# Last output projection in token rows: a per-token norm without a column sum and a spread

## What is computed

```python
def rmsnorm(x, gain):
    y = xf * lax.rsqrt(jnp.mean(xf * xf, axis=-1, keepdims=True) + RMS_EPS)
    return (y * gain.astype(jnp.float32)).astype(x.dtype)

def odd_mixer(h, w_in, pool_w, pool_scale, w_out):
    u, gate = jnp.split(h @ w_in, [POOL_WIDTH], axis=-1)          # 2048 each
    y = multiscale_pool(u, pool_w, pool_scale)
    return (y * jax.nn.silu(gate)) @ w_out                         # 256x2048 @ 2048x1024
...
        x = x + rmsnorm(y, post_norm[layer])                       # the result, 256x1024
```

## Time and profile before

| | us |
|---|---|
| median of 3 runs | 2239.26 (2237.56 to 2242.36) |
| the profiled execution, its own time | 2245.09 |
| its span | 2243.3 |
| PE busy | 2089.1 (93%) |
| PE weight loads busy | 1126.8 (50%) |
| DVE busy | 716.1 (32%) |
| ACT busy | 397.6 (18%) |
| POOL busy | 51.3 (2%) |
| DMA | 572.84 MB, mean 255 GB/s |

### The profile page before, as it was taken

How to read it: one execution, slowest core, us unless ns; L and a number is a source line. 1 busy time by engine, 2 the same in 40 slices (tenths; PEclk the granted TensorE clock), 3 DMA queues, 4 the chain that set the end, 5 groups by cost and what they waited for, 6 DMA issues and landing times.

```text
span 2243.3 us, 26279 instructions
## 1 busy us (share of the span) xinstructions
PE 2089.1 (93%) x10404; PEld 1126.8 (50%) x10404; DVE 716.1 (32%) x1732; ACT 397.6 (18%) x853; POOL 51.3 (2%) x70
## 2 busy tenths in 40 slices
PE   5999999996999999999799899999998999889997
PEld 2345447753334334334466533333333767578886
DVE  3035218625110110112447211111112697710411
ACT  2014210012110110111226211111111232411101
POOL 0000000001000000001000000000000000000000
PEclk9999999997999999999899899999999999798998
DMA  9661219212999999998630399999999633242230
GB/s 361 249 225 38 76 50 368 124 38 91 373 427 414 409 429 411 418 428 362 262 113 17 141 416 428 428 429 427 428 429 414 217 121 96 76 160 94 88 119 19
DMA packets 114475, 572.84 MB, mean 255 GB/s; under 512 B 6112, under 2 KB 20704, under 8 KB 89680
## 3 DMA queue, kind: packets, MB, share of 16 engines
q1 hardware_dynamic: 105280, 541.38, 60.1%
q0 software_dynamic: 6512, 24.67, 3.0%
q10 hardware_dynamic: 2592, 5.51, 0.6%
HBM read 562.88 MB, written 8.65 MB: 255 GB/s over the span
## 4 chain that ended last, share of the span: by engine, by line
PE 77%; DMA 11%; DVE 7%; ACT 2%; issue 2%; SPq 1%; POOL 0%; ACTq 0%; DVEq 0%; POOLq 0%; PEldq 0%
PE banks L516 26%; PE banks L982 7%; PE banks L920 4%; PE banks L960 4%; PE banks L1092 4%; DMA weight_ring<-in_moe_w_up 3%; DMA weight_ring<-in_moe_w_down 3%; PE banks L530 3%; PE banks L728 3%; DMA pages<-h_rows,pages 3%; DVE pages L1902 2%; PE banks L1046 2%; PE banks L937 2%; PE banks L1010 2%; PE banks L1078 2%; PE banks L708 2%
## 5 line engine op out<-in xcount | busy, mean ns | idle before, releaser
L516 PE MATMUL banks<-pages,weight_ring 128*128 128x256 f32 (+1 forms) x2240 | 579.6, 420 | 8.4 <-ACT pages L1601 3.2
L516 PEld LDWEIGHTS banks<-pages,weight_ring 128*128 128x128 f32 x2240 | 429.8, 193 | 157.1 <-issue 103.2
L982 PE MATMUL banks<-weight_ring,pages 128*64 128x512 f32 x992 | 224.0, 597 | 9.7 <-DMA weight_ring<-in_moe_w_gate 5.0
L1686 ACT ACTIVATE pages<-banks 128x512 f32<-128x512 f32 (+1 forms) x150 | 84.3, 572 | 688.6 <-PE banks L862 117.2
L1902 DVE TENSOR_TENSOR pages<-banks,pages 128x512 f32<-128x512 f32 (+3 forms) x165 | 95.4, 619 | 324.0 <-PE banks L890 182.4
L1576 ACT ACTIVATE pages<-banks 128x256 f32<-128x256 f32 (+2 forms) x216 | 91.9, 453 | 597.8 <-PE banks L516 421.7
L920 PE MATMUL banks<-weight_ring,pages 128*64 128x512 f32 x832 | 184.1, 598 | 3.2 <-issue 3.2
L1902 DVE TENSOR_TENSOR pages<-pages 128x512 f32<-128x512 f32 (+9 forms) x306 | 176.2, 598 | 9.2 <-issue 1.1
L1902 DVE TENSOR_TENSOR pages<-pages,banks 128x512 f32<-128x512 f32 (+1 forms) x41 | 28.2, 688 | 410.6 <-PE banks L982 178.0
L982 PEld LDWEIGHTS banks<-weight_ring,pages 128*64 128x64 f32 x992 | 69.0, 137 | 158.1 <-issue 132.5
L1092 PE MATMUL banks<-weight_ring,pages 128*64 128x512 f32 x512 | 114.9, 597 | 6.4 <-DVE pages L2359 5.4
(11 more groups left out here) (297 smaller groups left out, 1828.3 us busy)
## 6 DMA issues: line engine op xcount, KB each, us to landing
weight_ring<-in_moe_w_up SPq DMA_DIRECT2D x64, 2048.0 KB, 19.2
weight_ring<-in_moe_w_down SPq DMA_DIRECT2D x64, 2048.0 KB, 18.6
weight_ring<-in_moe_w_gate SPq DMA_DIRECT2D x62, 2048.0 KB, 17.6
weight_ring<-in_ada_w SPq DMA_DIRECT2D x24, 2048.0 KB, 15.9
weight_ring<-in_even_w_in SPq DMA_DIRECT2D x18, 2048.0 KB, 20.2
weight_ring<-in_odd_w_in SPq DMA_DIRECT2D x8, 2048.0 KB, 8.3
weight_ring<-in_odd_w_out SPq DMA_DIRECT2D x6, 2048.0 KB, 8.9
weight_ring<-in_odd_w_qkv SPq DMA_DIRECT2D x3, 2048.0 KB, 12.7
```

The source lines that it names most:

```text
L516: last = pe.matmul(b[:, 0:w], s[:, k, m * P:(m + 1) * P], src(k)[:, t0:t0 + w], start=(k == 0), stop=(k == nk - 1))
L982: last = pe.matmul(to, xg[:, par, k, 64 * half:64 * half + 64], rows, start=(half == 0 and k == 0), stop=(half == 1 and k == 3))
L1686: act.activation(dst, banks_mem[:, use(l, job)[0], 0:n], func).then_inc(moe_taken(l, job, 0)[0], 1)
```

## The change

- The residual `X` is turned into token rows (`x_tok`, page 2) by 16 PE transposes in four jobs between the pool projection and `out3`; ACT copies the four banks out.
- `out3` takes the activations as the stationary operand (128 tokens) and 256 columns of the weights as the moving one. Chunk c gives two jobs, tokens t = 0 and t = 1, of 128 tokens by 256 features.
- ACT squares each job's bank with a running sum per token into one column of `square_sums`; the squares themselves are not used. DVE multiplies the bank by the gain, which now lies along the row and is a new 128x1024 table (`post_row`), loaded by POOL behind the reciprocals; `recip_loaded` is waited for at 32 in the place of 16.
- In the last chunk, for each t: DVE adds the four sums and scales, ACT takes the root of a 128x1 column, DVE the reciprocal, and then y * r + x in two pieces of 128x512.
- SP stores each piece with a DMA of its own, 256 KB, as soon as it is counted in `x_final`.
- The ones-matmuls, the spread, the eight scalings, the eight adds and the transposes at the end go.

```diff
@@ PE
-        wait_taken(pe, ("pool", ("pool", 0, 3), 3))
-            project("b3o", ("out3", 0, c), lambda k: yp[:, k], 16, 2, NX, n=256)
-        columns_sum("norm_q1", pages(4, 4096).rearrange("p (k t) -> p k t", k=KT), KT, NX)
-        for half in range(2):
-            pe.wait_ge(sem("x_final"), 4 * (half + 1))
-            for s in range(2):
-                job = ("x_out", s, half)
+        for s in range(2):
+            for half in range(2):
+                job = ("x_tok", s, half)
                 b = open_job(job)
                 for k in range(4):
                     last = pe.transpose(b[:, k * P:(k + 1) * P], X[:, 4 * half + k, s * P:(s + 1) * P], ident)
                 close_job(job, last)
+        wait_taken(pe, ("pool", ("pool", 0, 3), 3))
+        for c in range(4):
+            name = ("out3", 0, c)
+            wait_weights(pe, name)
+            w_ = slot(name, 16, 256)
+            for t in range(2):
+                b = open_job(("b3o", name, t))
+                for k in range(16):
+                    last = pe.matmul(b[:, 0:256], yp[:, k, t * P:(t + 1) * P], w_[:, k], start=(k == 0), stop=(k == 15))
+                close_job(("b3o", name, t), last)
+            last_job[name] = ("b3o", name, 1)
@@ SP
-                wait_taken(sp, ("x_out", s, half))
-        sp.dma_start(out[0].rearrange("(s p) n -> p s n", p=P),
-                     pages(2).rearrange("p (s n) -> p s n", s=2)).then_inc(sem("stored"), 16)
-        sp.wait_ge(sem("stored"), 16)
+                sp.wait_ge(sem("x_final"), 2 * s + half + 1)
+                sp.dma_start(out[0, s * P:(s + 1) * P, 512 * half:512 * half + 512],
+                             x_tok[:, s, 512 * half:512 * half + 512]).then_inc(sem("stored"), 16)
+        sp.wait_ge(sem("stored"), 64)
@@ POOL
         put(pages(12, 1024, 1024), tab("recip"), "recip_loaded")
+        put(post_row, tab("post_row"), "recip_loaded")
@@ ACT
+        for s in range(2):
+            for half in range(2):
+                evac(("x_tok", s, half), x_tok[:, s, 512 * half:512 * half + 512])
         for c in range(4):
-            for m in range(2):
-                evac(("b3o", ("out3", 0, c), m), y_raw[:, 2 * c + m], NX)
-        squares("norm_q1", y_raw, 4, NX)
-        root("norm_q1", NX)
+            for t in range(2):
+                b = result(act, ("b3o", ("out3", 0, c), t))
+                act.activation(square_out[:, 2 * c + t], b[:, 0:256], ACT.Square, accum_out=square_sums[:, 4 * t + c:4 * t + c + 1])\
+                    .then_inc(sem("norm_squared"), 1)
+                if c == 3:
+                    act.wait_ge(sem("norm_root"), 2 * NORMS.index("norm_q1") + 2 * t + 1)
+                    act.activation(tok_root[:, t:t + 1], tok_root[:, t:t + 1], ACT.Sqrt).then_inc(sem("norm_root"), 1)
@@ DVE
-        dve.wait_ge(sem("recip_loaded"), 16)
+        dve.wait_ge(sem("recip_loaded"), 32)
...
-        add_normed("norm_q1", vec("post", 8, 8), "x_final")
-        o = pages(2).rearrange("p (s n) -> p s n", s=2)
-        for half in range(2):
-            for s in range(2):
-                evac(("x_out", s, half), o[:, s, 512 * half:512 * half + 512])
+        for c in range(4):
+            for t in range(2):
+                job = ("b3o", ("out3", 0, c), t)
+                cols = slice(256 * c, 256 * c + 256)
+                b = result(dve, job)
+                dve.wait_ge(sem("norm_squared"), KT * NORMS.index("norm_q1") + 2 * c + t + 1)
+                if c == 3:
+                    r = tok_root[:, t:t + 1]
+                    link(dve.reduce_sum(r, square_sums[:, 4 * t:4 * t + 4], AX.X))
+                    dve.tensor_scalar(r, r, 1.0 / D, EPS, ALU.mult, ALU.add).then_inc(sem("norm_root"), 1)
+                y_known = tt(y_tok[:, t, cols], b[:, 0:256], post_row[:, cols], ALU.mult)
+                y_known.then_inc(taken_sem(job), 1)
+                if c == 3:
+                    dve.wait_ge(sem("norm_root"), 2 * NORMS.index("norm_q1") + 2 * t + 2)
+                    link(dve.reciprocal(r, r))
+                    wait_taken(dve, job)
+                    for half in range(2):
+                        wait_taken(dve, ("x_tok", t, half))
+                        cols = slice(512 * half, 512 * half + 512)
+                        dve.scalar_tensor_tensor(x_tok[:, t, cols], y_tok[:, t, cols], r, x_tok[:, t, cols],
+                                                 ALU.mult, ALU.add).then_inc(sem("x_final"), 1)
```

More of the change, by code:

```diff
@@ L76 @@
     ("cos2", 256), ("sin2", 256), ("rot2", 128), ("dilated", 512),
-    ("iota", 256), ("rows", 2), ("recip", 1024),
+    ("iota", 256), ("rows", 2), ("recip", 1024), ("post_row", 1024),
     ("before", 128), ("slots", 512), ("turn", 80)])
@@ L432, in program @@
     y_raw = pages(11).rearrange("p (k t) -> p k t", k=KT)
+    y_tok = pages(11).rearrange("p (s n) -> p s n", s=2)
+    x_tok = pages(2).rearrange("p (s n) -> p s n", s=2)
+    post_row = pages(12, 1024)
+    square_out = pages(10).rearrange("p (i n) -> p i n", i=8)
+    square_sums = S("tiny", 8, 8)
+    tok_root = S("tiny", 0, 2)
     RS = pages(13, 128)
@@ L1359, in _ @@
             project("pool", ("pool", 0, g), lambda k: mixed[:, 4 * g + k], 4, 4, NX)
-        wait_taken(pe, ("pool", ("pool", 0, 3), 3))
-        yp = pages(4, 4096).rearrange("p (j t) -> p j t", j=16)
-        for c in range(4):
-            project("b3o", ("out3", 0, c), lambda k: yp[:, k], 16, 2, NX, n=256)
-        columns_sum("norm_q1", pages(4, 4096).rearrange("p (k t) -> p k t", k=KT), KT, NX)
-        for half in range(2):
-            pe.wait_ge(sem("x_final"), 4 * (half + 1))
-            for s in range(2):
-                job = ("x_out", s, half)
+        for s in range(2):
+            for half in range(2):
+                job = ("x_tok", s, half)
                 b = open_job(job)
@@ L1373, in _ @@
                 close_job(job, last)
+        wait_taken(pe, ("pool", ("pool", 0, 3), 3))
+        yp = pages(4, 4096).rearrange("p (j t) -> p j t", j=16)
+        for c in range(4):
[8 more added lines that the diff above has]
+            last_job[name] = ("b3o", name, 1)
     @block_.sync
@@ L2735, in _ssm, with _tabs @@
     return np.ascontiguousarray(np.concatenate([parts[n] for n in SSM], axis=1))
-def _tabs():
+def _tabs(a):
     t = {}
@@ L2798, in _tabs @@
     t["rows"] = (f[:, None] // 16 % 2 == np.arange(2)[None, :])
+    t["post_row"] = np.broadcast_to(a["post_norm_2"][1], (P, D))
     t["recip"] = np.concatenate(
@@ L2815 @@
     given = {name: np.ascontiguousarray(a[name]) for name in _INS}
-    given["vecs"], given["ssm"], given["tabs"] = _vecs(a), _ssm(a), _tabs()
+    given["vecs"], given["ssm"], given["tabs"] = _vecs(a), _ssm(a), _tabs(a)
     arrays, dram = {}, {}
```

## The result

The changed kernel takes 2225.94 us (median of 5 runs, 2222.52 to 2229.05), the kernel before 2239.26 (5 runs, 2237.56 to 2242.36): a ratio of 0.9939, 95% interval 0.9924 to 0.9954. That is 13.3 us faster by the medians, with an interval of about 10 to 17 us.

A forecast was written before the change was run, and what follows sets the result against it. PE holds 77% of the chain, but nothing remains to overlap in the last 20.85 us. Tail 20.85 - 6.1 = 14.75 saved, less 1.31 for a later projection, gives 13.4 off 2239.26: 2225.9 us, range 2222.4 to 2231.7.

The forecast's parts named there:

- PE ahead of the projection: Before the last projection: sixteen moved transposes take 1.89 us, cover a 0.58 wait for DVE, so it starts 1.31 later.
- The projection: Last projection on PE: 128 matmuls with only the stationary side changed, same time as before, 0 us.
- the rival of an exposed stationary side: Last projection: 256 activation loads of 0.19 us stop hiding beside matmuls, 48.6 us added, 2274.5; chance 2%.
- The new load: 512 KB gain table loaded on POOL, which DVE awaits before pooling: 0 us, with 59 us of cover.
- the four copies: ACT copies of turned residual during the last projection: 2.8 us inside 55.5, nothing on the path.
- the first half's norm: Norm of tokens 0 to 127: 4.3 us beside PE's last job of 6.9 us, costing nothing.
- The tail: From the last matmul's end to the end of the span: 6.1 us in place of 20.85.
- The landing of the last store: Last 256 KB store on SP lands in 2.5 us, bounds 2.2 and 4.0.
- the gain product: After the last matmul's end E, DVE multiplies the bank by the gain in 0.42 us, ending at E + 1.37.
- the dear store: Rival at the end: a 256 KB piece lands only after 4.0 us, gain 11.9, 2227.4; chance 10%.
- the table load: Rival: ACT reloads its table between last square and root, 1.28 us, costing 0.8, gain 12.6, 2226.7; chance 4%.
- The level case: Whole kernel comes out level: the untouched 2166 us before the tail shift by some 9 us; chance 3%.

The follow-up runs named there:

- together run: Changed kernel with the norm of both halves made together after the last matmul: stage (DVE's last pool instruction to span end) 64.50 us, +2.23.

## Why the prediction was right

Forecast 2225.9, measured 2225.94; the faster side, and the mechanism, were as forecast. That the medians meet to a tenth is luck: the stage gained 14.64, not 13.4, and runs differ by several us. From one profiled execution to the other the prediction said 2231.7, and it was 2224.52: 1.2 of the 7.2 us lie in the stage, 6.0 ahead of it, where nothing had been forecast. Step by step:

- *PE ahead of the projection*, 1.31 later: measured 1.01 (1.55 less 0.54), in the changed kernel and alone in the kernel before. The sixteen transposes took 1.75 from the first to the projection's start (2161.98 - 2160.23), 0.109 each at the full clock, in the place of 1.89: the 0.118 of the earlier trace rows counts the last one to its end, as the 1.92 here does. And they begin 0.20 before DVE's instruction (2160.43 - 2160.23), not the 0.04 of the prediction (2166.39 - 2166.35).
- *The projection*, 0: measured 55.42 against 55.52. The rival of an exposed stationary side found nothing: 256 weight loads were hidden beside the matmuls as before.
- *The new load, the four copies, the first half's norm*, 0 each: right, with the covers named; the first half's norm took 3.6 us (2210.53 to 2214.16), not 4.3. The together run shows what the last is worth when its cover is gone: 2.23.
- *The tail*, 6.1: measured 5.30 (2222.7 - 2217.40). The first scale-and-add starts 1.42 after PE's end, not 1.57; DVE ends at 2.84, not 3.08, for two overlapping instructions take 1.42 and not 2 x 0.753. The last issue is at 2.87. These are the small terms, 0.3 in all.
- *The landing of the last store*, 2.5: measured 2.0. This is the largest miss of a single term. I drew a line between a load of 199 KB and a store of 1 MB; the 256 KB store lies below that line, and below the estimate of 2.6 that the prediction set beside it. From the last landing to the end of the span remain 0.43, as forecast (5.30 - 2.87 - 2.0).

Together: 0.8 in the tail, 0.3 ahead of the projection and 0.1 in it are the 1.2 us between 13.4 and 14.64. Two slips in the prediction's sums change nothing: by its own terms the gain product ends at E + 1.39 and not 1.37, and the range takes the runs' spread with its sides exchanged. With 1.7 at the low end and 3.1 at the high one it is 2223.8 to 2233.1, and the measured median lies in that too.

What the old tail gave up is 15.55 us (20.85 - 5.30). The two timelines divide it, as the chain is serial in both:

| stretch | before | after | less |
|---|---|---|---|
| last matmul of the projection to the first scaling | 7.08 | 1.42 | 5.66 |
| from there to the first transpose, or the last issue where none follows | 4.85 | 1.45 | 3.40 |
| transposes and copies, to the issue of the store | 4.49 | 0 | 4.49 |
| issue to the end of the span | 4.43 | 2.43 | 2.00 |

The first row is the eight squares, the table load and PE's sum and spread against one square and sum per token; the second is eight scalings and the first four adds, for which PE's first transposes wait, against two scale-and-adds. Within this, two parts are shown by runs: 2.0 by the store's size, and 2.23 by the first half's norm beside PE's last job, nearly all of it in the first two rows. The other 11.3 us are read from the timelines; no run changed the layout alone.

Of the rivals, the dear store and the table load were each made to happen: they cost 1.91 and 0.83, where the prediction had 1.5 (it counted from a landing of 2.5) and 0.8. Neither happens in the changed kernel. The level case has a true core: executions do differ by some 6 us ahead of the stage.

## What to carry to other kernels

In a tail like this one the work is a single chain and nearly every instruction on it counts in full, so lay the last product out in the form in which it is stored: then the norm is one column per token, needs no matmul to sum or spread, and its first half runs beside the last matmuls. What the tail needs from elsewhere belongs ahead of it only for the part that is used before PE ends; PE is idle afterwards and did the rest for nothing here. Store the last piece small, here 256 KB, but not smaller, and measure a short stage inside the profile when the gain is less than the spread of whole runs.

## What was not expected of the hardware

- The landing of a store on SP's queue: 4.0 us for 1 MB, 2.0 to 2.1 for 256 KB and 2.1 for 128 KB. Below 256 KB nothing was gained.
- The old tail's own length differed with the clock: its sixteen transposes took 3.67 where the windows show a granted clock of 0.50 throughout, and 3.32 where the second half's window shows 0.76, with the same work in the tail before them. What brought the clock back sooner there is open.
